# Modulation vectors by VectorE's multiply-and-add over weights laid out by feature, and a first norm with four projections that go tile by tile

## What is computed

```python
def first_block(x, c, w_ada, b_ada, norm1_g, w_in, ...):
    mod = silu(c) @ w_ada[l] + b_ada[l]            # c: (1, 1024), w_ada: (1024, 6 * 1024)
    sh1, sc1, g1, sh2, sc2, g2 = split(mod, 6)     # six vectors of 1024
    h = rmsnorm(x, norm1_g[l]) * (1.0 + sc1) + sh1
    proj = h @ w_in[l]                             # q (8 heads), k, v (2 heads), u_pool (4 groups)
    q, k = rope(rmsnorm(q)), rope(rmsnorm(k))
    mix = concat([attention(q, k, v), pool_mixer(u_pool)]) @ w_out[l]
    x = x + g1 * mix
    h2 = rmsnorm(x, norm2_g[l]) * (1.0 + sc2) + sh2
    x = x + g2 * conv_gated_ffn(h2, w_up[l], conv_w[l], conv_b[l], w_down[l])
    return x
# second_block: six more such vectors from c_2 @ w_ada_2, sparse and stick-breaking attention, FFN of 4096
```

## Time and profile before

| | |
|---|---|
| median of 3 runs | 1462.77 us (1462.42 to 1463.26) |
| profiled execution | 1461.17 us, its span 1459.4 us |
| PE busy | 1403.2 us, 96% of the span |
| DVE, ACT, POOL busy | 827.5, 649.2, 705.6 us (57, 44, 48%) |
| mean granted clock of TensorE | 0.982 |
| read from HBM | 164.31 MB |

### The profile page before, as it was taken

One profiled execution on the slowest core, in us unless ns is written; L12 is line 12 of the kernel. 1 busy time (PEld: TensorE's weight loads), 2 busy tenths in 40 slices (PEclk: granted clock), 3 DMA queues, 4 the chain that ended last, 5 costly groups with the idle time before them and its releaser, 6 DMA issues.

```text
span 1459.4 us, 18453 instructions
## 1 busy us (share of the span) xinstructions
PE 1403.2 (96%) x7351; PEld 1181.1 (81%) x7351; DVE 827.5 (57%) x1289; ACT 649.2 (44%) x1199; POOL 705.6 (48%) x380
## 2 busy tenths in 40 slices
PE   6889999999999999999999999999999999999998
PEld 6668778988888888887877877888888888788886
DVE  5567746577878675656777976543366431202224
ACT  5355536434332341634677665456454322413231
POOL 1347554455555553653333454338806654635560
PEclk8899999999999999999999999999999999999999
DMA  9415532355556554331222321114311223222321
GB/s 334 135 56 171 176 111 93 114 204 185 180 186 211 174 198 157 110 86 58 59 58 58 87 58 58 59 59 144 102 44 59 87 90 112 87 87 87 103 99 58
DMA packets 133573, 167.59 MB, mean 115 GB/s; under 512 B 14192, under 2 KB 109040, under 8 KB 133488
## 3 DMA queue, kind: packets, MB, share of 16 engines
q1 hardware_dynamic: 133488, 166.42, 35.6%
HBM read 164.31 MB, written 2.10 MB: 114 GB/s over the span
## 4 chain that ended last, share of the span: by engine, by line
PE 85%; DVE 7%; ACT 4%; POOL 2%; issue 1%; DMA 1%; SPq 0%; DVEq 0%; ACTq 0%
PE B L553 82%; PE B L975 1%; ACT WH L1196 1%; PE B L785 1%; DVE SC L1784 1%; DVE ZF L1862 1%; DVE SC L2179 1%; DVE ZF L2154 1%; PE B L668 1%; POOL WL L2328 1%; DMA SC<-in_w_ada 1%; DVE SC L1951 0%; POOL G L2366 0%; DVE M L2152 0%; DVE ZR L2171 0%
## 5 line engine op out<-in xcount | busy, mean ns | idle before, releaser
L2328 POOL TENSOR_TENSOR WL<-RAW,WH 128x512 fp32r<-128x512 f32 (+1 forms) x197 | 468.9, 2394 | 501.6 <-ACT WH L1196 457.4
L553 PE MATMUL B<-HH,WH 128*128 128x512 f32 (+2 forms) x1040 | 404.8, 392 | 5.0 <-ACT HH L1282 2.1
L553 PE MATMUL B<-HH,WL 128*128 128x512 f32 (+2 forms) x1040 | 397.6, 385 | 0.0
L553 PE MATMUL B<-HL,WH 128*128 128x512 f32 (+2 forms) x1040 | 386.3, 383 | 0.0
L1196 ACT ACTIVATE WH<-RAW 128x512 fp32r<-128x512 f32 (+1 forms) x197 | 191.8, 1004 | 185.3 <-PE B L553 168.9
L553 PEld LDWEIGHTS B<-HH,WH 128*128 128x128 f32 x1040 | 197.1, 190 | 44.7 <-issue 4.3
L553 PEld LDWEIGHTS B<-HH,WL 128*128 128x128 f32 x1040 | 196.8, 189 | 39.0
L553 PEld LDWEIGHTS B<-HL,WH 128*128 128x128 f32 x1040 | 192.0, 189 | 34.5
L553 PE MATMUL B<-ZR 128*128 128x256 f32 (+4 forms) x1048 | 152.6, 328 | 16.1 <-ACT SC L1537 3.2
L553 PE MATMUL B<-ZR,WH 128*128 128x512 f32 (+1 forms) x624 | 164.9, 353 | 0.1
L553 PEld LDWEIGHTS B<-ZR 128*128 128x128 f32 (+1 forms) x1048 | 121.4, 192 | 42.9 <-issue 15.0
(11 more groups left out here) (246 smaller groups left out, 1855.7 us busy)
## 6 DMA issues: line engine op xcount, KB each, us to landing
ZF<-in_w_ada SPq DMA_DIRECT2D x84, 512.0 KB, 4.5
RAW<-in_w_ff SPq DMA_DIRECT2D x32, 1024.0 KB, 5.2
RAW<-in_w_up SPq DMA_DIRECT2D x22, 1024.0 KB, 5.1
RAW<-in_w_in SPq DMA_DIRECT2D x16, 1024.0 KB, 5.2
RAW<-in_w_in SPq DMA_DIRECT2D x19, 512.0 KB, 5.1
RAW<-in_w_down SPq DMA_DIRECT2D x8, 1024.0 KB, 5.2
G<-in_w_ada SPq DMA_DIRECT2D x8, 512.0 KB, 10.2
RAW<-in_w_out SPq DMA_DIRECT2D x4, 1024.0 KB, 5.1
```

The costliest lines, as they stand in the source:

```text
L553: return e.matmul(out, l, r, start=start, stop=stop)
L2328: e.tensor_tensor(lo[:, at], k.RAW[:, i % 2, at], hi[:, at].bitcast(F32), ALU.subtract).then_inc(*w.hit((i, q)))
```

## The change

The host now passes x transposed, and w_ada with its rows and columns exchanged, so that a chunk (j, m) holds for each of the 128 features of tile m all 1024 weights. DVE spreads c over all partitions once (CR, made by 16 transposes on PE and four copies) and gets the 128 values of tile m of a vector with one `tensor_tensor_reduce` (`summed`): multiply the chunk by CR, add along the row. It compiles to two instructions, the long one and a read of the accumulator. No transposes and no reductions follow. All twelve vectors go this way except tiles 0 to 3 of the shift (vector 0), which PE does from a block in the old orientation (`shift_tile`).

The first norm's squares are summed over features by PE, and scale, shift, HH and HL are made tile by tile (`first_sum`, `first_gain`, `unit`, `rounded`, `first_low`). PE takes q0k and q1v together as the tiles come (`rows_of`), then q2, q3 and p0 before the attention begins. Slab q23 gets a place of its own. The chunks of vectors 2, 4 and 3 now stand, eight each, in the head chain (points "0"), in attention steps 9 to 30, and behind residuals 0 to 3 (points "2"). Near the end, ACT copies the two coefficient rows (ROT) within the third group of the second FFN (at ch 17) and not behind it.

```diff
+def turned(a):
+
+    w = np.asarray(a["w_ada"][0])
+    return {"xt": np.ascontiguousarray(np.asarray(a["x"][0]).T), "w_ada": np.ascontiguousarray(w.T),
+            "w_ada_2": np.ascontiguousarray(np.asarray(a["w_ada_2"][0]).T),
+            "w_turned": np.ascontiguousarray(w[:, 0:128 * TURNED].reshape(8, 128, TURNED, 128).transpose(2, 1, 0, 3)
+                                             .reshape(128 * TURNED, 1024))}
...
-ADA = [(j, k) for j in (1, 0) for k in range(8)] + [(j, k) for k in range(8) for j in (4, 2)]
-ADA += [(j, k) for j in (3, 5, 6, 7, 8, 9, 10, 11) for k in range(8)]
-EARLY = 16
...
+ADA = [(j, m) for j in (2, 4, 3, 5, 6, 7, 8, 9, 10, 11) for m in range(8)]
+
+FIRST = [(j, m) for m in range(8) for j in (1, 0)]
+PLACES = 6
+TURNED = 4
...
-T1 = {"q3": 0, "p0": 5, "p1": 10, "p2": 15, "p3": 20}
...
-SPLIT1 = {t + q: q for t in (0, 8, 14, 28) for q in range(4)}
+T1 = {"p0": -4, "p1": 5, "p2": 9, "p3": 13}
+
+POOL_OUT = {19: 0, 21: 1, 23: 2, 25: 3}
+
+SPLIT1 = {t + q: q for t in (0, 14, 28) for q in range(4)}
...
-        many = {"1": 8 <= p < 32, "2": 0, "gate": 2, "val": 2, "down": 2 - point[1]}[g]
...
+        many = {"0": 2, "1": p in range(9, 33, 3), "2": 2, "gate": 2, "val": 2, "down": 2 - point[1]}[g]
...
-    def first_slab(name, keys, st):
-
-        wh, wl = slab(name)
-        bs = [B.take(pe, "main", key) for key in keys]
+    def rows_of(name, keys, lo, hi):
+
+        bs = [B.take(pe, "main", key) if lo == 0 else B[key] for key in keys]
         for i, b in enumerate(bs):
-            for j in range(8):
-                pe.wait_ge(hh[st, j])
+            for j in range(lo, hi):
+                wh, wl = slab(name, j)
+                pe.wait_ge(hh[0, j])
                 mm(b[:, :], wh[:, j, 128 * i:128 * i + 128], HH[:, j, :], j == 0, False)
                 mm(b[:, :], wl[:, j, 128 * i:128 * i + 128], HH[:, j, :], False, False)
         for i, b in enumerate(bs):
-            for j in range(8):
-                pe.wait_ge(hl[st, j])
+            for j in range(lo, hi):
+                wh, _ = slab(name, j)
+                pe.wait_ge(hl[0, j])
                 t = mm(b[:, :], wh[:, j, 128 * i:128 * i + 128], HL[:, j, :], False, j == 7)
-            t.then_inc(*proj_full.hit(keys[i]))
-        spend(name, keys[1])
+            if hi == 8:
+                t.then_inc(*proj_full.hit(keys[i]))
+        if hi == 8:
+            spend(name, keys[1])
...
+    def shift_tile(m):
+
+        b = B.take(pe, "shift", ("shift", m))
+        n = FIRST.index((0, m))
+        pe.wait_ge(k.sig(f"in_first{n % PLACES}")[n])
+        for kt in range(8):
+            t = mm(b[:, m:m + 1], k.place[n % PLACES][:, 128 * kt:128 * kt + 128], k.CA[:, kt:kt + 1],
+                   kt == 0, kt == 7)
+        t.then_inc(*ada_full.hit((0, m)))
...
+    first = (("q0k", ("q0", "k")), ("q1v", ("q1", "v")))
+    shift_tile(1)
+    rows_of(*first[0], 0, 1)
+    shift_tile(2)
+    rows_of(*first[0], 1, 2)
+    shift_tile(3)
+    rows_of(*first[0], 2, 3)
+    rows_of(*first[1], 0, 3)
+    for m in range(3, 8):
+        rows_of(*first[0], m, m + 1)
+        rows_of(*first[1], m, m + 1)
...
-    first_slab("q0k", ("q0", "k"), 0)
-    head("q0")
-    proj("q1", "q1v", 0, hx, 0, 3)
-    head("k")
-    proj("q1", "q1v", 0, hx, 3, 6)
-    head_rows("q0")
-    proj("q1", "q1v", 0, hx, 6)
-    proj("v", "q1v", 128, hx, 0, 2)
-    head_rows("k")
-    proj("v", "q1v", 128, hx, 2)
-    spend("q1v", "v")
-    head("q1")
-    proj("q2", "q23", 0, hx, 0, 4)
...
+    proj("q2", "q23", 0, hx, 0, 2)
+    head("q0", "hd")
+    proj("q2", "q23", 0, hx, 2, 4)
+    head("k", "hd")
+    proj("q2", "q23", 0, hx, 4, 7)
+    head_rows("q0", "hd")
+    proj("q2", "q23", 0, hx, 7)
+    proj("q3", "q23", 128, hx, 0, 1)
+    head_rows("k", "hd")
+    proj("q3", "q23", 128, hx, 1, 3)
+    head("q1", "hd")
+    proj("q3", "q23", 128, hx, 3, 6)
+    b = B.take(pe, "hd", ("tok", "v"))
     pe.wait_ge(a_mix["tok", "v"])
     for q in range(4):
         t = e.transpose(b[:, 128 * q:128 * q + 128], k.slot(9)[:, 128 * q:128 * q + 128], k.IDN)
     t.then_inc(*tok_full.hit("v"))
-    proj("q2", "q23", 0, hx, 4)
+    proj("q3", "q23", 128, hx, 6)
+    spend("q23", "q3")
+    proj("p0", "p01", 0, hx, ring="p")
...
-        for n in k.chunks["1", s]:
-            if by_pe(*ADA[n]):
-                ada_chunk(n, "a")
-        for j in k.sums["1", s]:
-            if j != 2:
-                ada_sum(j, ("t", "t"))
...
+    quarters(1, 4)
+    rounded(0)
+    rounded(1)
+    quarters(0, 2)
+    rounded(2)
+    quarters(2, 4)
+    rounded(3)
+    rounded(4)
+    rounded(5)
+    quarters()
+    act.wait_ge(k.sig("in_cst")[0])
     for half in range(2):
         for v in (k.VH, k.VL):
             e.activation(heads_of(v[half])[1 - half], heads_of(k.CST[:, 0:512])[0], ACT.Copy, scale=0.0).then_inc(
                 *mix.hit("fill"))
-    weights()
-    for j in range(8):
-        act.wait_ge(v_ada["gain", 0])
-        act.wait_ge(v_h["unit", j])
-        e.activation(k.slot(j), k.slot(j), ACT.Copy, scale=k.GS[:, 0, j:j + 1]).then_inc(*sq.hit(("gain", 0, j)))
-    for j in range(8):
-        act.wait_ge(sq["gain", 0, j])
-        act.wait_ge(v_ada["mod", 0])
-        e.activation(k.HH[:, j, :], k.slot(j), ACT.Identity, bias=k.MOD[:, 0, j:j + 1]).then_inc(*hh.hit((0, j)))
+    rounded(6)
+    rounded(7)
...
+            if ch == 17:
+                for part in range(2):
+                    act.wait_ge(out_full["coef", part])
+                    e.activation(k.ROT[:, part, :], B["coef", part][:, :], ACT.Copy).then_inc(*post.hit(("coef", part)))
+                    B.free(("coef", part), post["coef", part])
...
+    def summed(j, m, src):
+        c = (16 + 8 * j if j < 6 else 292 + 8 * (j - 6)) + m
+        e.tensor_tensor_reduce(out=src, in0=src, in1=k.CR[j // 6], scale=1.0, scalar=k.VT[:, c:c + 1], op0=ALU.mult, op1=ALU.add,
+                               accum_out=k.MOD[:, j, m:m + 1]).then_inc(*ada.hit((j, m)))
+        if m == 7:
+            ada.also(("mod", j))
...
-            e.tensor_scalar(dst, src, c, None, ALU.mult).then_inc(*ada.hit((j, kt)))
-        else:
-            dve.wait_ge(ada[j, kt - 1])
-            e.scalar_tensor_tensor(out=dst, in0=src, scalar=c, in1=dst, op0=ALU.mult, op1=ALU.add).then_inc(*ada.hit((j, kt)))
...
+    first_gain(0)
+    unit(0)
+    unit(1)
+    for m in range(1, 8):
+        first_sum(1, m)
+        if m >= TURNED:
+            first_sum(0, m)
+        first_gain(m)
+        if m < 7:
+            unit(m + 1)
+        first_low(m - 1)
+    first_low(7)
...
     head_newton("q0")
     head_newton("k")
+    ada_point(("0", 0))
     head_scaled("q0")
     head_scaled("k")
+    ada_point(("0", 1))
     rotated("q0", *QKS["q0"][:2])
     rotated("k", *QKS["k"][:2])
+    ada_point(("0", 2))
     head_newton("q1")
+    ada_point(("0", 3))
...
-        if m == 3:
-            ada_point(("2", 0))
+        if half is None:
+            ada_point(("2", m))
...
+    def first(n):
+
+        j, m = FIRST[n]
+        if n >= PLACES:
+            old = FIRST[n - PLACES]
+            sp.wait_ge((ada_full if old[0] == 0 and old[1] < TURNED else v_ada)[old])
+        src = a["w_turned"][128 * m:128 * m + 128, :] if j == 0 and m < TURNED else a["w_ada"][1024 * j + 128 * m:1024 * j + 128 * m + 128, :]
+        load(f"in_first{n % PLACES}", n, k.place[n % PLACES], src)
...
+            sp.wait_ge(v_ada[ADA[n - 2] if n > 1 else FIRST[n + 12]])
+            at = 1024 * (j % 6) + 128 * m
+            load(f"in_ada{n % 2}", n, k.chunk[n % 2], a["w_ada" if j < 6 else "w_ada_2"][at:at + 128, :])
...
+    first(0)
+    first(1)
     weights()
-    for n in range(10, EARLY):
-        ada(n)
+    for n in range(2, PLACES):
+        first(n)
     weights()
+    for n in range(PLACES, 16):
+        first(n)
+    weights()
+    load("in_cst", 0, k.CST[:, 128:576], a["consts"][:, 128:576])
     rot(0)
-    ada(16)
-    ada(17)
     weights()
-    weights()
+    ada(0)
+    ada(1)
+    for p in range(4):
+        for n in k.chunks["0", p]:
+            ada(n + 2)
...
+    for m in range(4):
+        for n in k.chunks["2", m]:
+            ada(n + 2)
```

292 lines of the change are left out of this document (117 added, 175 removed).

## The result

The changed kernel takes **1482.72 us** (median of 4 runs, 1481.25 to 1484.13) against 1462.6 (1459.56 to 1463.26) for the kernel before, run beside it: a ratio of **1.0139**, 95% interval 1.0125 to 1.0153. It is slower by 20 us where I forecast 18.9 less; its profiled span is 1481.5 against 1459.4. The rival that I had put on this side, a sum in two passes, is not what happened, though its number, 1482, is the one that was measured: that is luck.

The account below looks back on a forecast made before the run. PE, busy 96% of the span, was taken as the bound, so work off it saves time. From 1461.2 us profiled, +8.3 - 31.2 + 15 - 6 - 5 = -18.9 gave 1442, or 1444 as a median; range 1427 to 1468.

Parts of the forecast that it names:

- a sum in two passes: DVE's sums throughout the kernel: each takes 2.5 us and not 1.35, 38 us more in total, 1482; chance 0.12.
- Part 2: Attention, with the wait behind unit 15: work taken off PE's list saves 31 us.
- 3 for DVE: Attention: allowance of 3 us for DVE being late, within the 76.4 from first exponential to unit 15.
- my own sign of being wrong: Attention: the forecast is wrong if units without weighing take 6 us, where about 4.2 was taken.
- Rival 2: Attention: gives back only 10, as DVE's chain fills the room that PE leaves; 1465, chance 0.13.
- Part 1: Start to the first exponential: 8 us later, at 89.7 where it was 81.43.
- norm term: First norm at the start: tiles 6 and 7 start near 49, heads q0 and k whole at about 55 us.
- the start would be cheaper: Start: q0 and k whole at 46, DVE's and POOL's work side by side; 1435, chance 0.12.
- Part 3: Entry to the FFN: 15 us more, gate 0 being issued only behind chunk 25, which waits for the last sum.
- Part 4: FFNs: 6 us less for transposes leaving PE, 5 less for the ROT copy moved ahead.
- the tail behind unit 15: End of the attention: 7.5 us less, from the fourth pool mean's wait, a pool matmul, transposes and half clock.
- The term that I bounded from both sides: DVE's sum of 1024 columns: taken as 1.35 us with the accumulator's read, between 1.3 and two passes of 1.3.

Follow-up runs that it names:

- e11: Changed kernel with p1 and p3 projected into a second PSUM bank, the spacing of four steps kept: 1472.4 us, ratio 1.0063.
- e17: e13 without the fourth score bank, q3's normalisation started four steps later and its projection kept in q2's bank: 1444.8 us, ratio 0.9870.
- e9: Changed kernel with the projections p1 to p3 five steps apart again and the pool matmuls two steps later: 1468.9 us, ratio 1.0042.
- e8: Changed kernel with the 24 sums ahead of the FFN over 64 columns instead of 1024, chunks still transferred: 1473.2 us, ratio 1.0068.
- e3: Changed kernel with ACT doing tiles 6 and 7 of the first norm ahead of rounding slab q23 and filling v: 1480.0 us, ratio 1.0117.
- e2: Changed kernel with SP issuing slab p23 behind the first two head-chain chunks instead of behind chunk 9: 1473.4 us, ratio 1.0080.
- e1: Changed kernel with the eight chunks behind residuals 0 to 3 moved into the attention, which then has 16: 1465.1 us, ratio 1.0013.
- b1: Kernel before with only ACT's ROT copy moved to after channel 17 of the second FFN: 1458.2 us, ratio 0.9965.
- e13: Changed kernel with the five edits of e1, e2, e3, e6 and e9 together: 1444.8 us, ratio 0.9870 to the kernel before.
- e7: Changed kernel with 45 useless matmuls added to PE's list in the attention, three behind each unit's scores from unit 1: 1484.4 us, ratio 1.0145.
- e10: Changed kernel with the four edits of e1, e2, e3 and e6 together: 1453.4 us, ratio 0.9933 to the kernel before.
- e6: Changed kernel with the attention's scores going round four PSUM banks instead of three: 1479.3 us, ratio 1.0109.
- e12: Changed kernel with the spacing of five steps of e9 and the four score banks of e6 together: 1465.7 us, ratio 1.0027.
- e14: e13 with 28 useless matmuls on PE between p0 and the scores of unit 0: 1445.9 us, ratio 0.9876.

## Why the prediction was wrong

**Part 2 is the step that failed.** I took PE for the bound of the attention, counted what of a unit "remains" on PE, scores, turn and weighing, and forecast 23.7 less for the work taken off it; the attention became 2.4 longer. The 26.1 between them lie in two places.

(1) Units 0 to 4: forecast 15.5 behind the first exponential, measured 28.3. The trace of before had 25.3 there, and PE was not full in it even with all of the 48 matmuls: 5.5 us of the 8.4 in which it idles in the attention are in this window of before.

```profile
81.40:106.70 25.30, 19.82 (x125) 15.71 (x123) 17.29 (x36) 13.80 (x34) 11.24 (x8) 1.00 0.19 52
```

I looked for waits near the end of the attention and overlooked these. Under PE's work another chain was running: the heads' normalisation through ACT and DVE, and q3's bank, which p1 wants (e11, e17). They account for up to 7.4 of the 12.8 (28.6 in e9, 21.2 in e17); what holds the rest is open.

(2) Units 4 to 15: forecast 57.9 and 3 for DVE, measured 74.2. The change also moved p1 to p3 from every fifth step to every fourth. I put them into the sum as 1.4 a step and never asked what their one PSUM bank and the POOL means between them need. e9, which restores the spacing, has 60.9, which is the forecast with its 3: so here the terms were right and the moved steps were left out. Units without weighing, which I had at 4.2 to 5.0, take 4.7 in the mean in e9 and 5.9 in the changed kernel, and 6 was my own sign of being wrong.

Rival 2 (the attention gives back only 10) was nearest for this stage, with DVE as its mechanism; DVE's maximum, low parts and sums weigh something (e8: 7.8), but the larger part was ACT behind POOL, and PE behind a bank.

**Part 1 was under-sized.** Its mechanisms are all in the trace. Its norm term was 6 short: q23 was issued at 40.48 and not at 34, and ACT stood for it until 50.22, ahead of tiles 6 and 7 (e3: 4.7 back). The first `unit` (L1782) stands at 22.60 and not at 18: the norm's sums over features are 64 matmuls with one column, which hold PE from 7.59 to 18.1, and I had them at nothing. The head chain, 34.7 forecast from q0 and k whole to the first exponential, took 37.4, since two of its sums ran 2.3 and 2.0 us and chunks were waited for four times. I had treated SP's order as given, though moving p23 in it is worth 9.3 in the median (e2). A rival said that the start would be cheaper; only the two-pass sum had it dearer.

**Part 3's mechanism holds** (e1: 18.4 of 19.9), at 19.9 for 15. The last sum ends at t + 21.1 and not t + 19.0, two of them taking 2.4 and 2.3 beside POOL's four subtractions, and gate 0 lands 7.2 behind its issue and not 5.9.

**Part 4 and the tail behind unit 15 were right:** -9.5 for -11, -7.9 for -7.5; of Part 4 the ROT copy is 5.0 (b1). The term that I bounded from both sides, the sum's duration, is 1.28 and 0.08, as taken. But its mean over the 84 chunks that pass through ZF is 1.68, with single ones up to 5.16, and each one above 1.4 runs beside an instruction of POOL (as do some of the short ones). One of my two bounds was wrong: that nothing reads 1024 columns in less than the multiply-and-add's 1.3 does not hold in the trace of before, where a multiply with one tensor source (L1859) takes 0.76.

By the rule of the Trainium skill that I cited (Vector Engine (DVE) Microarchitecture Reference, section 7), the sum would have had half its throughput. The trace does not agree: 1024 fp32 columns from two SBUF sources, with the accumulator, in 1.28 us, the same as the multiply-and-add without it in the earlier trace rows.

Open is what the fourth score bank is worth beside 16 sums (e13 and e17 differ in more than that).

The start differs between executions of kernels with the same instructions there, and the traces show where: in PE's first 40 one-column matmuls of the norm. The changed kernel, then e7:

```profile
7.59 5.42 PE L547 MATMUL B<-ONES,SC 128*128 128x1 f32 x40
```
```profile
7.59 8.53 PE L547 MATMUL B<-ONES,SC 128*128 128x1 f32 x40
```

They take 5.4 to 5.6 in the changed kernel, e1, e2, e3, e9, e10, e11 and e13, and 8.53 in e6, e7, e8, e12 and e14 to e17. Without e3's edit the first head's square stands at 58.7 to 61.4 in the first group and at 63.2 to 65.9 in the second; with it, at 56.5 and at 60.5 to 61.0. So this costs 3 to 4 us, and a comparison across the groups is blurred by as much; e13 against e14 to e17 is one. At 0.21 each these matmuls have the pace of the half clock (16 of them take 3.55 in the changed kernel too, where its clock is down), though the clock column of the second group reads 1.00 there; why the clock rose in some executions and not in others is not shown.

## What to carry to other kernels

An engine that is 92% busy in the mean of a stage is not proven to be its bound: look for its waits in every part of the stage, and before counting work taken off it as time, follow one round of the slowest chain through the other engines' lists, and see what it would need with that engine free. Where a change also moves steps of a hand-written schedule, price each moved step by the buffer that it waits for and by who waits behind it in the copying engine's list; here two small tables were worth 14 us, more than all that left PE in the FFNs. And small transfers in one in-order DMA queue, each waiting for its consumer, hold back every slab behind them: issue the slab first, or spread the small ones over a stage that has room.

## What the runs showed that I had not expected

The same instructions, with three projections four steps apart or five, make an attention of 102.5 or 89.4 us. Where other engines set the pace, the half clock cost nothing of its own: with 28 idle matmuls ahead of the scores TensorE had 1.00 instead of 0.73 in the window before them, and the attention took 86.8 instead of 87.2. Where PE sets the pace it does cost: 3.1 us on the 40 matmuls of the first norm, which go on to the first exponential. DVE's sum, shortened from 1024 to 64 columns, is 0.28 us, so by the two lengths some 0.2 us of it do not depend on the columns.
